# One encoder layer with 16 experts: the third expert list ahead moved behind the row transposes, and a head transpose moved behind the second pool product

## The chip, the cores and the metric

The kernel runs on one core of a Trainium2 chip. A core has a matrix engine (TensorE, called PE in the profile, with its weight loads as PEld), a vector engine (VectorE, DVE), a scalar engine (ScalarE, ACT), a general engine (GpSimd, POOL) and a queue engine (SyncE, SP). Each works through its own list of instructions in order. They meet only through semaphores. Transfers between the main memory and the on-chip buffers run on 16 DMA engines. SP and POOL issue them.

The metric is the device time of one execution in microseconds (us), and less is better. All times "from the start" are counted from the start of the profiled span.

## The reference

One layer for 576 tokens: 512 prompt rows and 64 rows of a running stream. The two groups are computed apart in the reference and together in the kernel.

```python
h = rmsnorm(x, g_mix); proj = h @ w_in                 # u, q, k, v
pool_out = multiscale_pool(u, ...)                     # 4 groups, each with its own 128x128 map
o = differential attention(q, k, v), 4 heads
x = x + concat([pool_out, attn_out]) @ w_out           # the out projection
h2 = rmsnorm(x, g_ffn)
expert_id, top_w = two of 16 experts for each token    # group of 4, then 2 in the group
for e in range(16):
    he = silu(h2 @ w_gate[e]) * (h2 @ w_up[e])         # 1024 -> 256
    moe = moe + combine[..., e:e+1] * (he @ w_down[e]) # 256 -> 1024
y = rmsnorm(x + moe, g_final)
```

## The kernel before

Each engine has a program written out by hand in one long function. The order of the instructions on an engine is the order of that code. A `wait_ge(semaphore, count)` holds the engine, with all that stands behind it, until another engine has counted that far.

**The out projection.** Tokens are worked in five tiles t = 0..4 of 128 (the last has 64). `project_out(t, half, features)` on PE multiplies one tile by one half (512 columns) of `w_out`. For each 128 features it makes three matmuls (lines 822, 823, 824), since both operands are split in a high and a low part. Features 0 to 3 are the pool outputs (`pools`), 4 to 7 the attention heads (`heads`). Four pool products stand among these calls. `pool_product(g)` (line 1014, two matmuls) writes banks 4 and 5 of PSUM. Before g > 0 it waits for `pool_evac`, which says that the banks have been read: first ACT writes the high part (line 1517) and then DVE the low part (`pool_lo`, line 1882). `transpose_o(3)` (line 986, four transposes) waits for `o_ready`, which DVE gives when it has scaled the attention rows of token tile 3 (`o_norm`, line 1813) with a factor that POOL makes in a chain of small steps (lines 645 to 655). ACT and DVE then write the transposed rows as high part (`oT_hi`, line 1491) and low part (`oT_lo`, line 1822).

**The expert loop.** 16 steps i = 0..15, unrolled for 0 to 3 and 12 to 15, a hardware loop between. An expert works on up to 128 token rows. Its tokens are named by a list that the kernel makes on the way:

- DVE makes a 0/1 table with the slots of the tokens (`expert_onehot`, line 2018).
- PE multiplies it with a table of token numbers and weights (`slot_lists` called by `lists_of`, line 1175, five small matmuls).
- DVE turns the product into the list (`lists_out`, lines 2122 and 2123), which counts `idx_ready`.
- POOL then issues an indirect DMA that fetches the rows (`gather_h2`, line 699, `region_x<-h_rows,lists`).

PE in step i: `gate_up` of expert i (line 1188, 64 matmuls), `transpose_rows` of the rows of expert i+1 (line 1181, eight transposes, waiting for the gather), `down_split` of expert i-1 (lines 1205, 1206, 1210) and `lists_of(3)`, the list of expert i+3. Step 1 makes two lists more, behind its `gate_up`. In step 1 `lists_of(3)` may not start before DVE has read the list of expert 2, since both use one PSUM bank.

DVE in step i: `he_out(i)` (lines 2129 to 2131, the product of gate and up), the one-hot table of expert i+3, from step 6 on `finish_row(i-2)` (lines 2152 to 2162, the final norm), `add_rows(i-1)` (line 2146: adds the weighted rows of expert i-1 to the sums gathered for them, so it waits for `down_split` and for a gather), `lists_out(i+3)`, `wd_los(i+1)` (line 2136). Step 0 ends with `count_overflow` (lines 2086 to 2112, 24 small instructions, once). Step 1 makes the lists of experts 2 and 3 besides.

POOL in step i, in this order: `gather_h2(i+3)`, from step 6 on two stores of finished rows (line 742, 743), `store_acc(i-1)` (waits for `add_rows`), `gather_acc(i+1)` (the sums that `add_rows(i+1)` needs). SP loads the weights of the experts up to four ahead: gate and up when the buffer is free behind `gate_up`, down behind `down_split`.

Of the kernel before, what the change touches and what calls it, by code (L numbers as in the profile page):

```python
# [54 lines left out]
E = G * EPG  # L55
# [10 lines left out]
EARLY = 3  # L66
# [21 lines left out]
def build(nc, x_prompt, x_sample, cache_k, cache_v, state_pool, g_mix, w_in, w_pool, pool_scale,  # L88
# [4 lines left out]
    with ctx:  # L93
# [712 lines left out]
        def _(pe):  # L806
# [277 lines left out]
            pool_product(0)  # L1084
            project_out(1, 0, heads[0:2])
            transpose_o(PT - 1)
            pool_product(1)
            project_out(1, 0, heads[2:4])
            project_out(1, 1, heads[0:1])
# [147 lines left out]
            def expert(it, u, left):  # L1237
# [21 lines left out]
                if first:  # L1259
                    pe.wait_ge(tab_ready, 1)  # L1260
                    for n in range(2):
                        lists_of(n)
                if not first and left != 0:
                    pe.wait_ge(he_ready, i)
                    if not (isinstance(it, int) and i == 1):
                        pe.wait_ge(added, i - 1)
                    pe.wait_ge(wd_lo_ready, i)
                    down_split((u - 1) % RING, i - 1, 4)
                if not first and (left is None or left >= EARLY):
                    lists_of(EARLY)  # L1270
                if left == 1:
# [45 lines left out]
        def _(act):  # L1317
# [197 lines left out]
            for g in range(H):  # L1515
                act.wait_ge(pool_full, g + 1)
                act.activation(two_halves(mix_hi[:, g, :]), ps[:, 4:6, 0:HALF], ACT.Copy,
                               scale=pscale[:, g:g + 1]).then_inc(pool_hi_ready, 1)
                if g == 0:
                    oT_hi(NT - 2)  # L1520
# [124 lines left out]
        def _(dve):  # L1645
# [239 lines left out]
            w_out_los(H)  # L1885
            w_out_los(H + 1)
            o_norm(NT - 2)
            pool_lo(0)
            w_out_los(H + 2)
# [281 lines left out]

            for i in range(E - 1):
                he_out(i)
                if i == 0:
# [3 lines left out]
                    lists_out(1)  # L2178
                if i == 1:
                    lists_out(2)  # L2180
                    lists_out(3)
                if i >= 1 and i + EARLY < E:
                    expert_onehot(i + EARLY)
                if i > RING + 1:
                    finish_row(i - 2)
                if i >= 1:
                    add_rows(i - 1)
                    if i + EARLY < E:
                        lists_out(i + EARLY)
                if i < E - 2:  # L2190
# [125 lines left out]
```

## Time and profile before

| | |
|---|---|
| device time, median of 3 runs | 452.24 us (451.46 to 453.07) |
| the profiled execution, its own time | 450.83 us |
| its span (first to last instruction in the trace) | 449.0 us |
| mean granted TensorE clock | 0.975 |
| PE busy | 421.5 us (94%) |
| DVE / ACT / POOL busy | 273.3 / 197.7 / 125.9 us |
| DMA moved | 91.36 MB, of it 18.93 MB by POOL's software queue |

PE is busy 94% of the span, so what matters is where PE waits, and where it runs at the lower of its clocks. In the trace's rows a bracket behind an instruction gives the idle time of its engine before it, and what ended it: `[1.50 <-DVE region_t L1813]` says that the engine was idle for 1.50 us until line 1813 of DVE had written region_t. Names like region_t stand for stretches of the on-chip memory that several tiles share. In the rows of this kernel region_x<-h_rows is the gather of token rows, ps is PSUM.

### The profile page before, as it was taken

What the parts mean: (1) busy time and instruction counts of PE and PEld (TensorE: products, weight loads), DVE (VectorE), ACT (ScalarE), POOL (GpSimd) and SP (SyncE); (2) the same over time, 40 slices, a digit from 0 to 9 for tenths busy, and PEclk for the clock granted to TensorE, in tenths of its full rate; (3) what the DMA queues carried; (4) which work ended last, traced back from release to release, by engine and by line L of the source; (5) the groups of instructions that cost most, each with busy time, mean ns of one, the idle gap of its engine ahead of it and who ended that gap; (6) DMA issues with size and microseconds to landing.
All of it is one profiled execution on the core that took longest, in us unless ns stands there. A gap on an engine that the chain in (4) does not pass through costs nothing.

```text
span 449.0 us, 7775 instructions
## 1 busy us (share of the span) xinstructions
PE 421.5 (94%) x2927; PEld 366.0 (82%) x2927; DVE 273.3 (61%) x655; ACT 197.7 (44%) x485; POOL 125.9 (28%) x207
## 2 busy tenths in 40 slices
PE   7899999999999998999998999999999998999970
PEld 3786999997876866888895988999999997899950
DVE  3855232616778987364258796555577775497770
ACT  6475222505576664232124433344455554366340
POOL 2010000200242415251001304333335543466431
PEclk9999999999999999999998999999999999899995
DMA  7841605306000089613226599998899999963120
GB/s 268 302 160 47 223 1 182 111 1 195 1 1 2 1 334 364 261 52 149 89 93 244 178 403 392 379 361 352 354 360 355 344 369 352 349 231 120 55 81 21
DMA packets 32073, 91.36 MB, mean 203 GB/s; under 512 B 11200, under 2 KB 11712, under 8 KB 27942
## 3 DMA queue, kind: packets, MB, share of 16 engines
q1 hardware_dynamic: 20790, 71.97, 43.4%
q0 software_dynamic: 11248, 18.93, 12.0%
q8 instruction: 21, 0.34, 0.3%
q14 instruction: 14, 0.11, 0.1%
HBM read 86.38 MB, written 26.01 MB: 250 GB/s over the span
## 4 chain that ended last, share of the span: by engine, by line
PE 61%; issue 12%; DVE 7%; POOL 7%; DMA 6%; ACT 5%; POOLq 0%; SPq 0%; DVEq 0%; ACTq 0%
PE ps L1188 13%; PE ps L822 9%; PE ps L824 9%; PE ps L823 9%; DMA region_x<-h_rows,lists 5%; PE ps L1125 2%; PE ps L1181 2%; PE ps L1205 2%; PE ps L1206 2%; PE ps L1210 2%; PE ps L943 2%; PE ps L978 2%; POOL region_x L699 2%; DMA region_x<-in_x_prompt 1%; POOL mix L699 1%
## 5 line engine op out<-in xcount | busy, mean ns | idle before, releaser
L1188 PE MATMUL ps<-region_p,region_a 128*128 128x128 f32 x512 | 59.1, 276 | 0.6 <-DVE region_p L2025 0.6
L1188 PEld LDWEIGHTS ps<-region_p,region_a 128*128 128x128 f32 x512 | 57.9, 192 | 1.2 <-DVE region_p L2025 1.1
L824 PE MATMUL ps<-region_a_r,region_w_r 128*128 128x288 f32 x192 | 56.5, 294 | 0.0
L699 POOL DMA_INDIRECT region_x<-h_rows,lists x13 | 22.1, 1700 | 77.6 <-DVE slot_w L2123 77.6
L822 PE MATMUL ps<-region_a_r,ring_r 128*128 128x288 f32 x128 | 40.5, 317 | 0.0
L823 PE MATMUL ps<-region_a_r,ring_r 128*128 128x288 f32 x128 | 37.7, 295 | 0.0
L1575 ACT ACTIVATE region_p<-ps,gffn_sb 128x128 f32<-128x128 f32 x116 | 31.5, 382 | 10.9 <-PE ps L1181 10.9
L824 PEld LDWEIGHTS ps<-region_a_r,region_w_r 128*128 128x128 f32 x192 | 36.1, 188 | 0.0
L1596 ACT ACTIVATE region_t<-ps 128x256 f32<-128x256 f32 x16 | 6.1, 382 | 56.1 <-PE ps L1188 56.1
L1188 PE MATMUL ps<-region_p,ring 128*128 128x128 f32 x256 | 29.6, 277 | 0.6 <-DVE region_p L2047 0.4
L822 PEld LDWEIGHTS ps<-region_a_r,ring_r 128*128 128x128 f32 x128 | 24.0, 188 | 6.9 <-issue 3.3
L1188 PEld LDWEIGHTS ps<-region_p,ring 128*128 128x128 f32 x256 | 28.9, 192 | 0.7 <-DVE region_p L2047 0.5
L1188 PE MATMUL ps<-region_p,region_w 128*128 128x128 f32 x256 | 29.5, 276 | 0.0
L2146 DVE SCALAR_TENSOR_TENSOR mix<-ps,slot_w,mix 128x1024 f32<-128x1024 f32 x15 | 19.2, 1282 | 16.4 <-DMA mix<-summed_rows,lists 10.8
L1188 PEld LDWEIGHTS ps<-region_p,region_w 128*128 128x128 f32 x256 | 29.0, 192 | 0.1
L1762 DVE TENSOR_SCALAR region_q<-ps 128x288 f32<-128x288 f32 x8 | 3.7, 458 | 39.8 <-PE ps L824 39.8
L2129 DVE TENSOR_TENSOR region_t_r<-region_t,ps 128x256 fp32r<-128x256 f32 x16 | 6.7, 421 | 32.7 <-ACT region_t L1596 32.7
L823 PE MATMUL ps<-region_w_r,mix_r 128*128 128x512 f32 x64 | 25.6, 399 | 0.0
L1205 PE MATMUL ps<-region_q_r,region_t_r 128*128 128x512 f32 x60 | 25.3, 421 | 0.0
L823 PEld LDWEIGHTS ps<-region_a_r,ring_r 128*128 128x128 f32 x128 | 24.1, 188 | 0.0
L1438 ACT ACTIVATE region_p<-ps,negm 128x128 f32<-128x128 f32 (+4 forms) x40 | 20.7, 527 | 5.8 <-DVE negm L1794 5.8
L1602 ACT ACTIVATE region_q<-mix 128x1024 f32<-128x1024 f32 x11 | 11.6, 1057 | 21.4 <-DVE mix L2146 21.4
(358 smaller groups left out, 1025.8 us busy)
## 6 DMA issues: line engine op xcount, KB each, us to landing
region_a<-in_w_gate SPq DMA_DIRECT2D x8, 1024.0 KB, 8.3
region_a<-in_w_up SPq DMA_DIRECT2D x8, 1024.0 KB, 13.2
region_a<-in_w_down SPq DMA_DIRECT2D x8, 1024.0 KB, 14.7
region_w<-in_w_in SPq DMA_DIRECT2D x2, 2048.0 KB, 10.2
region_w<-in_w_out SPq DMA_DIRECT2D x2, 2048.0 KB, 8.0
ring<-in_w_gate SPq DMA_DIRECT2D x4, 1024.0 KB, 9.2
ring<-in_w_up SPq DMA_DIRECT2D x4, 1024.0 KB, 13.9
ring<-in_w_down SPq DMA_DIRECT2D x4, 1024.0 KB, 13.1
```

The lines of the kernel that those rows point to most:

```text
L699: pool.indirect_dma_start(out=dst, out_offset=None, in_=src, in_offset=bass.IndirectOffsetOnAxis(ap=at, axis=0), bounds_check=bound[n], oo ...
L822: pe.matmul(out, lhs_hi, rhs_hi, start=first, stop=False)
L823: pe.matmul(out, lhs_hi, rhs_lo, start=False, stop=False)
L824: return pe.matmul(out, lhs_lo, rhs_hi, start=False, stop=last)
L943: ins = pe.matmul(ps[:, b + c, 0:(t + 1) * P], q, kT[r, h, 0:(t + 1) * P], start=True, stop=True)
L978: ins = pe.matmul(ps[0:m, O_BANK[t], h * VD:(h + 1) * VD], aT[0:keys, n % 2, k * P:k * P + m], v, start=(k == 0), stop=(k == len(tiles) - 1))
L1188: ins = pe.matmul(ps[:, 2 + b, (first + c) * P:(first + c + 1) * P], w[:, k, c * P:(c + 1) * P], xT[:, b, k, :], start=(k == 0), stop=(k = ...
L1205: pe.matmul(ps[:, bank + half, :], he_hi[:, b, c, :], w_hi[:, c, n], start=(c == 0), stop=False)
L1438: ins = act.activation(prob[0:m, n % 2, c, 0:w], ps[0:m, 2 * (n % 2) + c, 0:w], ACT.Exp, bias=negm[0:m, n % 2, c:c + 1], scale=-1.0, accum ...
L1575: return act.activation(xT[:, b, k, :], ps[:, k // 4, (k % 4) * P:(k % 4 + 1) * P], ACT.Copy, scale=gffn_sb[:, k:k + 1])
L1602: act.activation(squares, xacc[:, i % RING, :], ACT.Square, accum_out=ssq[:, i % 2:i % 2 + 1]).then_inc(squared, 1)
L2146: dve.scalar_tensor_tensor(acc, ps[:, bank:bank + 2, :], slot_w[:, w:w + 1], acc, ALU.mult, ALU.add).then_inc(added, 1)
```

## The change

Two parts. In the out projection the second half of `project_out(1, 0, heads)` moves ahead of pool product 1, and `transpose_o(3)` moves behind it. ACT and DVE follow in their order: `oT_hi(3)` behind the second pool product's high part, `pool_lo(0)` ahead of `o_norm(3)`.

In the expert loop PE makes `lists_of(3)` right behind `transpose_rows`, ahead of `down_split`. DVE makes the list right behind `he_out`, ahead of the one-hot table, `finish_row` and `add_rows`. The one-hot tables are made one step earlier, which puts that of expert 4 into step 0, and the lists of experts 2 and 3 stand ahead of `he_out(1)`.

```diff
             project_out(0, 1, heads[2:4])
             pool_product(0)
-            project_out(1, 0, heads[0:2])
+            project_out(1, 0, heads)
+            pool_product(1)
             transpose_o(PT - 1)
-            pool_product(1)
-            project_out(1, 0, heads[2:4])
             project_out(1, 1, heads[0:1])
             pool_product(2)
...
+                if not first and (left is None or left >= EARLY):
+                    lists_of(EARLY)
                 if not first and left != 0:
                     pe.wait_ge(he_ready, i)
...
                     down_split((u - 1) % RING, i - 1, 4)
-                if not first and (left is None or left >= EARLY):
-                    lists_of(EARLY)
...
-                if g == 0:
+                if g == 1:
                     oT_hi(NT - 2)
...
             w_out_los(H + 1)
+            pool_lo(0)
             o_norm(NT - 2)
-            pool_lo(0)
             w_out_los(H + 2)
...
             for i in range(E - 1):
+                if i == 1:
+                    lists_out(2)
+                    lists_out(3)
                 he_out(i)
                 if i == 0:
...
-                if i == 1:
-                    lists_out(2)
-                    lists_out(3)
-                if i >= 1 and i + EARLY < E:
-                    expert_onehot(i + EARLY)
+                elif i + EARLY < E:
+                    lists_out(i + EARLY)
+                if i + EARLY + 1 < E:
+                    expert_onehot(i + EARLY + 1)
                 if i > RING + 1:
                     finish_row(i - 2)
                 if i >= 1:
                     add_rows(i - 1)
-                    if i + EARLY < E:
-                        lists_out(i + EARLY)
```

PE in the out projection, from behind the first part of `project_out(1, 0, heads)` to pool product 2. L986 is `transpose_o(3)`, L1014 a pool product, L822 to L824 the projection. Before:

```order
L986 MATMUL ps<-ident,region_t 128x128 x4
L1014 MATMUL ps<-mix,region_x 128x288 x2
L822 MATMUL ps<-region_x_r,mix_r 128x512
L823 MATMUL ps<-region_w_r,mix_r 128x512
L824 MATMUL ps<-region_x_r,region_a_r 128x512
L822 MATMUL ps<-w_hi_extra,mix_r 128x512
L823 MATMUL ps<-region_w_r,mix_r 128x512
L824 MATMUL ps<-w_hi_extra,region_a_r 128x512
L822 MATMUL ps<-ring_r,mix_r 128x512
L823 MATMUL ps<-region_w_r,mix_r 128x512
L824 MATMUL ps<-ring_r,region_a_r 128x512
L1014 MATMUL ps<-mix,region_x 128x288 x2
```

After, the same stretch:

```order
L822 MATMUL ps<-region_x_r,mix_r 128x512
L823 MATMUL ps<-region_w_r,mix_r 128x512
L824 MATMUL ps<-region_x_r,region_a_r 128x512
L822 MATMUL ps<-w_hi_extra,mix_r 128x512
L823 MATMUL ps<-region_w_r,mix_r 128x512
L824 MATMUL ps<-w_hi_extra,region_a_r 128x512
L1014 MATMUL ps<-mix,region_x 128x288 x2
L986 MATMUL ps<-ident,region_t 128x128 x4
L822 MATMUL ps<-ring_r,mix_r 128x512
L823 MATMUL ps<-region_w_r,mix_r 128x512
L824 MATMUL ps<-ring_r,region_a_r 128x512
L1014 MATMUL ps<-mix,region_x 128x288 x2
```

Six projection matmuls stand ahead of pool product 1 now, the transposes stand behind it, and only three matmuls and the transposes stand between pool products 1 and 2.

PE in step 1 of the expert loop, from its `gate_up`. L1188 (L1187 after) is `gate_up`, L1175 (L1174) a list product, L1181 (L1180) `transpose_rows`, L1205 and L1206 (L1204 and L1205) the start of `down_split(0)`. Before:

```order
L1188 MATMUL ps<-region_p,region_a 128x128 x32
L1175 MATMUL ps<-region_q,region_v 128x8 x10
L1181 MATMUL ps<-ident,region_x 128x128 x8
L1205 MATMUL ps<-region_q_r,region_t_r 128x512
L1206 MATMUL ps<-ring_r,region_t_r 128x512
```

After:

```order
L1187 MATMUL ps<-region_p,region_a 128x128 x32
L1174 MATMUL ps<-region_q,region_v 128x8 x10
L1180 MATMUL ps<-ident,region_x 128x128 x8
L1174 MATMUL ps<-region_q,region_v 128x8 x5
L1204 MATMUL ps<-region_q_r,region_t_r 128x512
L1205 MATMUL ps<-ring_r,region_t_r 128x512
```

The list product x5 stood behind the whole of `down_split(0)` and stands ahead of it now.

DVE from the end of `count_overflow` (step 0) through step 1. L2129 to L2131 is `he_out(1)`, L2122 and L2123 are a list, L2018 is a one-hot table, L2146 `add_rows(0)`. Before:

```order
L2112 CAST ctl<-region_k 1x1
L2129 TENSOR_TENSOR region_t_r<-region_t,ps 128x256
L2130 TENSOR_TENSOR region_t<-region_t,ps 128x256
L2131 TENSOR_TENSOR region_t_r<-region_t,region_t_r 128x256
L2122 TENSOR_SCALAR lists<-ps 128x4
L2123 TENSOR_REDUCE slot_w<-ps 128x1
L2122 TENSOR_SCALAR lists<-ps 128x4
L2123 TENSOR_REDUCE slot_w<-ps 128x1
L2018 TENSOR_TENSOR region_v<-iota_one,rm 128x640
L2146 SCALAR_TENSOR_TENSOR mix<-ps,slot_w,mix 128x1024
L2122 TENSOR_SCALAR lists<-ps 128x4
L2123 TENSOR_REDUCE slot_w<-ps 128x1
```

After (each of these lines has a number lower by one):

```order
L2111 CAST ctl<-region_k 1x1
L2121 TENSOR_SCALAR lists<-ps 128x4
L2122 TENSOR_REDUCE slot_w<-ps 128x1
L2121 TENSOR_SCALAR lists<-ps 128x4
L2122 TENSOR_REDUCE slot_w<-ps 128x1
L2128 TENSOR_TENSOR region_t_r<-region_t,ps 128x256
L2129 TENSOR_TENSOR region_t<-region_t,ps 128x256
L2130 TENSOR_TENSOR region_t_r<-region_t,region_t_r 128x256
L2121 TENSOR_SCALAR lists<-ps 128x4
L2122 TENSOR_REDUCE slot_w<-ps 128x1
L2017 TENSOR_TENSOR region_v<-iota_one,rm 128x640
L2145 SCALAR_TENSOR_TENSOR mix<-ps,slot_w,mix 128x1024
```

The two lists stand ahead of `he_out(1)`, but still behind `count_overflow`; the list of expert 4 stands ahead of the one-hot table and `add_rows`. Ahead of `count_overflow` the one-hot table of expert 4 has come in, between the lists of step 0 and `wd_los(1)`:

```order
L2121 TENSOR_SCALAR lists<-ps 128x4
L2122 TENSOR_REDUCE slot_w<-ps 128x1
L2017 TENSOR_TENSOR region_v<-iota_one,rm 128x640
L2135 TENSOR_TENSOR region_a_r<-region_a,region_q_r 128x1024 x2
L2085 TENSOR_SCALAR region_k<-region_k 128x16
```

Before, no L2018 stood there.

## Rows read from the trace of the kernel before

**Rows 1.** The page: costliest groups (busy, mean ns | idle before) and DMA issues (us to landing).

```profile
L699 POOL DMA_INDIRECT region_x<-h_rows,lists x13 | 22.1, 1700 | 77.6 <-DVE slot_w L2123 77.6
...
region_a<-in_w_down SPq DMA_DIRECT2D x8, 1024.0 KB, 14.7
```

**Rows 2.** Timeline of PE in the out projection: start us, us, engine line op [idle before].

```profile
172.62 0.61 PE L822 MATMUL ps<-ring_r,mix_r 128*128 128x512 f32 x1
...
175.88 0.66 PE L986 MATMUL ps<-ident,region_t 128*128 128x128 f32 x4 [1.50 <-DVE region_t L1813]
176.70 1.35 PE L1014 MATMUL ps<-mix,region_x 128*128 128x288 f32 x4 [0.16 <-DVE region_a_r L1882]
...
181.40 1.13 PE L1014 MATMUL ps<-mix,region_x 128*128 128x288 f32 x4
182.16 0.61 PE L822 MATMUL ps<-ring_r,mix_r 128*128 128x512 f32 x1
...
184.46 1.13 PE L1014 MATMUL ps<-mix,region_x 128*128 128x288 f32 x4
185.21 0.61 PE L822 MATMUL ps<-region_p_r,mix_r 128*128 128x512 f32 x1
```

**Rows 3.** Timelines of DVE, then of ACT, in the same stretch.

```profile
175.14 0.69 DVE L1813 TENSOR_TENSOR region_t<-ps,osc 128x512 f32<-128x512 f32 x1 [1.49 <-POOL osc L655]
...
178.87 0.82 DVE L1882 SCALAR_TENSOR_TENSOR region_a_r<-ps,pscale,mix_r 128x576 fp32r<-128x576 f32 x1 [1.19 <-ACT mix_r L1517]
...
173.30 0.73 ACT L1517 ACTIVATE mix_r<-ps,pscale 128x576 fp32r<-128x576 f32 x1
...
178.09 0.74 ACT L1517 ACTIVATE mix_r<-ps,pscale 128x576 fp32r<-128x576 f32 x1 [0.83 <-PE ps L1014]
```

**Rows 4.** Windows: stretch, us, busy by engine, then PEclk, DMA share, GB/s.

```profile
176.50:181.50 5.00, 4.84 (x15) 3.80 (x15) 2.66 (x4) 1.43 (x2) 0.00 (x0) 0.66 0.97 378
```

**Rows 5.** Windows of four steps of the expert loop, from one gate_up to the next.

```profile
272.95:284.45 11.50, 11.23 (x94) 10.34 (x92) 5.59 (x9) 4.53 (x11) 4.44 (x4) 1.00 1.01 380
...
306.41:317.39 10.98, 10.98 (x95) 10.32 (x92) 5.67 (x9) 4.55 (x11) 3.77 (x3) 1.00 0.98 396
...
372.68:387.92 15.24, 12.81 (x95) 11.75 (x92) 9.94 (x23) 5.58 (x13) 7.07 (x6) 0.89 0.97 379
387.92:399.25 11.33, 11.23 (x95) 10.36 (x93) 6.27 (x15) 5.70 (x13) 4.50 (x4) 1.00 0.71 245
```

**Rows 6.** Timeline of PE in the expert loop: first rows behind its waits.

```profile
261.50 4.73 PE L1188 MATMUL ps<-region_p,region_a 128*128 128x128 f32 x40 [0.65 <-DVE region_p L2025]
...
280.62 1.09 PE L1181 MATMUL ps<-ident,region_x 128*128 128x128 f32 x8 [0.27 <-DMA region_x<-h_rows,lists]
...
382.50 1.97 PE L1181 MATMUL ps<-ident,region_x 128*128 128x128 f32 x8 [2.43 <-DMA region_x<-h_rows,lists]
```

**Rows 7.** Tile h_rows on POOL, 331 to 367: the four gathers for steps 8 to 11.

```profile
L699 POOL DMA_INDIRECT region_x<-h_rows,lists x4: 1727/1736/1738, 331.8 to 366.2; - x4
...
DMA to landing us min/median/max: 9.1/12.6/16.2
```

**Rows 8.** Timeline of DVE in the expert loop, steps 6 and 10.

```profile
326.03 0.42 DVE L2131 TENSOR_TENSOR region_t_r<-region_t,region_t_r 128x256 fp32r<-128x256 f32 x1
...
331.41 0.15 DVE L2123 TENSOR_REDUCE slot_w<-ps 128x1 f32<-128x3 f32 x1
...
378.85 1.28 DVE L2146 SCALAR_TENSOR_TENSOR mix<-ps,slot_w,mix 128x1024 f32<-128x1024 f32 x1 [4.39 <-DMA mix<-summed_rows,lists]
```

**Rows 9.** Timeline of DVE from the end of count_overflow, then of PE, step 1.

```profile
270.33 0.14 DVE L2112 CAST ctl<-region_k 1x1 int32<-1x1 f32 x1
...
271.67 0.15 DVE L2123 TENSOR_REDUCE slot_w<-ps 128x1 f32<-128x3 f32 x1
...
271.94 0.82 DVE L2018 TENSOR_TENSOR region_v<-iota_one,rm 128x640 bf16<-128x640 f32 x1
...
269.83 0.47 PE L1205 MATMUL ps<-region_q_r,region_t_r 128*128 128x512 f32 x1
```

## The prediction

> **What bounds the kernel now.** I read the busy times first: PE works 94% of the span, so the time is PE's work, plus its waits, plus what it loses at the lower clock. Then the page's groups, for who waits on whom: the gathers of token rows cost POOL little, but POOL idles 77.6 us in front of them, all of it for DVE's lists [rows 1]. The DMA issues give the landing of a weight load, 14.7 us for the down weights [rows 1]. Then PE's timeline at the two places that the change touches.
>
> In the out projection PE idles 1.50 us for the scaled head rows of tile 3 (line 1813) and 0.16 us for pool product 0's banks [rows 2]. DVE was not late by its own work there: it idled 1.49 us for POOL's factor [rows 3]. From 176.5 to 181.5 the granted clock is 0.66 of full [rows 4], which is a stretch at 1.2 GHz within one at 2.4 GHz. It follows that idle.
>
> In the expert loop an undisturbed step takes 10.98 us. Three steps take longer: step 2 11.50, step 11 15.24, step 12 11.33, that is 0.52 + 4.26 + 0.35 = 5.13 us too much [rows 5]. The rows behind the waits name the cause: the transposes of step 2 waited 0.27 us for their gather, those of step 11 2.43 us [rows 6]. Behind the second wait the clock fell too (0.89 in that step's window [rows 5], and the eight transposes took 1.97 us where they took 1.09 in step 2 [rows 6]). So of step 11's 4.26 us some 2.4 are waiting, and the other 1.8 (mainly the clock) come behind it. I take 1.6 us as what one fall of the clock costs PE in this loop.
>
> The gathers get later from step to step: from issue to landing 9.1 us for the first of the four behind 331, 16.2 us for the last, issued at 366.2 [rows 7]. That is (16.2 - 9.1) / 3 = 2.4 us a step, with the DMA engines at a share of 0.97 to 1.0 [rows 5]. The last lands at 366.2 + 16.2 = 382.4. PE was ready for it at 382.50 - 2.43 = 380.07 [rows 6].
>
> **Part 1, the out projection.** Before, the stretch from the projection at 172.62 to the projection with the pool features at 185.21 takes 12.59 us [rows 2]. What it takes now:
>
> - Nine projection matmuls take 184.46 - 182.16 = 2.30 us [rows 2]; twelve take 3.0. So pool product 1 can start at 172.62 + 3.0 = 175.6. Its banks are free by then: ACT has written the high part by 173.30 + 0.73 = 174.0, and DVE, idle until 175.14, can write the low part (0.82) by 174.9 [rows 3]. The wait of 0.16 goes.
> - A pool product takes 182.16 - 181.40 = 0.76 us until the next matmul starts [rows 2]. The transposes come at 176.4. Their rows are there at 175.88 [rows 2], because POOL's factor is as early as before. The wait of 1.50 goes: six matmuls and a pool product cover it.
> - The transposes and three matmuls end at about 177.7. Pool product 2 needs the banks of product 1. Product 1 takes 1.13 [rows 2] and is done at 176.7; then ACT's 0.74 and DVE's 0.82 in a row [rows 3] make 178.4 to 178.5. **A new wait of 0.8 us** stands there, where nine matmuls at the lower clock hid it before.
> - From pool product 2 to product 3 it is 184.46 - 181.40 = 3.06, and 0.75 more to the pool features [rows 2]: 178.5 + 3.06 + 0.75 = 182.3.
>
> Gain: 185.21 - 182.33 = **2.88 us**. It assumes that the wait of 0.8 does not bring the lower clock. If it does, the three matmuls behind it run as they do in the stretch of 0.66 [rows 4], and 1.6 us come back. Everything behind stands on PE, so the 2.88 shift the rest as a whole.
>
> **Part 2, the lists.** In step 6 `he_out` ends at 326.45 and the list at 331.56 [rows 8]. Between them stood the one-hot table, the final norm and `add_rows`. The list now comes right behind `he_out`: about 4.9 us earlier, and so does the gather that waits for it. In step 10 `add_rows` waited 4.39 us for a gather of its own [rows 8], which held the list of step 12's rows too; this hold goes as well. POOL's stores stand behind the gather and follow by some 3 us, as the final norm ends at nearly its old time.
>
> What the earlier issue is worth depends on the queue. If the transfer takes as long as before, step 11's rows land at 382.4 - 4.9 = 377.5, 2.6 us ahead of the need. It takes only 2.4 of the 4.9 to end that wait. Step 12 is the tighter one: its gather ended just as PE came for it, at a time when PE was 5 us late; to be in time without that delay, it must land about 4.3 us earlier than before. Bounds for what is left there: 0 and 2 us; I take 0.6, nearer to the low end, since its issue comes earlier by more than 4.9. So of the 5.13 us the change takes **4.5**. Step 2's part goes because PE comes there later now (next paragraph).
>
> **Part 2, the new wait in step 1.** This is the cost. `lists_of(3)` of step 1 needs the bank that DVE frees with the list of expert 2. This list stands behind `count_overflow`, which ends at 270.33 + 0.14 = 270.47 [rows 9]. The one-hot table of expert 4 now stands in front of all that, and DVE has no idle there: 0.8 us [rows 9] make it 271.25, and the two small instructions of a list 271.5. PE reaches the place where `down_split` started, 269.83 [rows 9], and stands until about 271.5 with the whole of `down_split(0)` and `gate_up(2)` queued behind. Cost: **1.65 us**. Before, the list product came 3 us later and waited for nothing.
>
> **The clock behind it.** The row of before is nearest in the two cases: an idle of 1.50 + 0.16 us [rows 2] was followed by the lower clock [rows 4], one of 2.43 us too; one of 0.65 us was not [rows 6]. A wait of 1.65 is nearer to the first. I take **1.6 us** for it; the other end is 0.
>
> Other edits: `lists_of(3)` and the one-hot tables only change places in the other steps. The list product needs a bank that was read a step ago and a table that was made a step ago, so PE waits for neither. The two lists ahead of `he_out(1)` delay `down_split(1)` by nothing, as that comes a step later. Bounds for the list product's place: 0.1 us a step either way over ten steps; I take 0.
>
> **Sum**, in the profiled execution: -2.88 - 4.53 + 1.65 + 1.6 = -4.16, so 450.83 - 4.16 = 446.7. That execution lies 1.41 us below the median of the three runs; against the median it is 452.24 - 4.16 = **448.1**.
>
> **The rivals.**
>
> - *The clock does not fall in step 1* (B): 448.1 - 1.6 = 446.5. For it: the wait stands at the edge of what the rows show.
> - *The clock falls at the new wait of 0.8* (E): 448.1 + 1.6 = 449.7. Against it: 0.65 us of idle brought nothing [rows 6].
> - *The queue and not the list sets when rows land* (C). For it: the gathers' time to land grows by 2.4 us a step, while PE and the lists keep their pace [rows 7], and the DMA engines are full [rows 5]. A gather issued earlier then only lies longer in the queue. I work it out with half the shift lost: step 11 keeps about 1.2 of its 2.43 us, step 12 up to 1, and one more fall of the clock comes in half the cases: 0.6 becomes 3.5, and the time 448.1 + 2.9 = 451.0. Against it: until 366 the gathers were issued only after the list, with POOL idle in front of them [rows 1], so the queue had time in which it was fed late.
> - *The gathers go ahead of the weights, and PE waits for weights* (D), which ends slower. Weights of down are asked for at the end of a step and needed two steps on, 22.0 us, and take 14.7 [rows 1]: 7.3 us of cover. If the 2.4 us a step that the gathers lost until now [rows 7] fall on the weights, three of the six steps from 6 on use up the cover, and the other three cost 2.4 us each, 7.1 in all, with one fall of the clock: -2.88 - 5.13 + 1.65 + 1.6 + 7.1 + 1.6 = +3.9, so 456.2. It decides from the point at which a weight load takes over 22 us. Against it: the cover is used up only if all of that growth changes sides.
>
> The Trainium skill, "DMA: Bandwidth & Descriptors", section "Queues, rings and completion order", says that each DMA engine goes in turns, packet by packet, through the queues for which it has work. By that rule POOL's queue keeps its share beside SP's weights however early it is filled, which is rival C, 451.0; this trace agrees in so far as the gathers slow down beside full engines, and does not show which queue gives way.
>
> **How the numbers follow.** A measurement of this kernel can tell about 0.3% from no change, 1.36 us. Chances: the forecast 448.1: 0.42; B 446.5: 0.24; E 449.7: 0.09; C 451.0: 0.18; D 456.2: 0.07. The range goes from B without the 0.6 and with 0.4 of the list product's bound, 445.5, to C with 0.4 of it, 451.4. D and the ends beyond are left out. Faster by over 0.3% (under 450.9): the forecast, B, E and about a third of C, 0.80. Within: the rest of C, 0.13. Slower: D, 0.07.
>
> **What would show it.** Right: no wait at line 986's transposes, a wait of about 0.8 us at pool product 2 for `pool_lo(1)`; in step 1 a wait of 1.4 to 1.7 us at the list product (L1174) for DVE's list, and the clock low behind it; no wait over 0.5 us at the transposes of steps 2 and 11; lists about 5 us earlier against `gate_up`. Wrong: the transposes of step 11 still wait over 1 us (C), `gate_up` waits for weights (D), the first part gains under 2 us because the clock falls there (E), or the stretch at the lower clock comes at another place of the loop that none of these rows shows.

## The result: 446.1 us, and the profile after

The changed kernel takes 446.14 us (median of 4 runs, 444.89 to 447.15) where the kernel before takes 452.65 us beside it: a ratio of 0.9848, 95% interval 0.9814 to 0.9883. A second set of runs, on another occasion (e5 below), gives 446.6 against 451.22 us, a ratio of 0.9884, interval 0.985 to 0.9918. So the change saves some 4.6 to 6.5 us by the medians. 448.1 us had been forecast, 2 us too much; the rival without a lower clock in step 1, 446.5 us, lies nearest. The times alone do not decide between the two, since they stand for gains of 4.2 and 5.8 us; the traces do.

The page of the changed kernel, its span and the group of the gathers:

```profile
span 443.2 us, 7774 instructions
...
L699 POOL DMA_INDIRECT region_x<-h_rows,lists x13 | 16.6, 1280 | 48.6 <-DVE slot_w L2122 48.2
```

The profiled execution is 5.8 us shorter in its span. POOL idles 48.6 us ahead of the gathers where it idled 77.6 [rows 1]: the lists do come earlier.

PE's timeline in the out projection, the rows that answer to [rows 2]:

```profile
172.33 0.61 PE L822 MATMUL ps<-ring_r,mix_r 128*128 128x512 f32 x1
...
175.31 1.13 PE L1014 MATMUL ps<-mix,region_x 128*128 128x288 f32 x4
176.28 0.60 PE L986 MATMUL ps<-ident,region_t 128*128 128x128 f32 x4
...
178.23 1.21 PE L1014 MATMUL ps<-mix,region_x 128*128 128x288 f32 x4 [0.65 <-DVE region_a_r L1881]
...
181.32 1.13 PE L1014 MATMUL ps<-mix,region_x 128*128 128x288 f32 x4
182.08 0.61 PE L822 MATMUL ps<-region_p_r,mix_r 128*128 128x512 f32 x1
```

The transposes (L986) have no idle in front of them. The wait has moved to pool product 2 and is 0.65 us long. The stretch takes 182.08 - 172.33 = 9.75 us; it took 12.59.

Windows of that stretch and of steps 1, 2, 11 and 12 of the expert loop (stretch, us, busy by engine, PEclk, DMA share, GB/s), the answer to [rows 5]:

```profile
172.33:182.08 9.75, 9.10 (x43) 7.05 (x41) 6.99 (x8) 3.47 (x5) 3.28 (x8) 1.00 1.02 374
258.36:271.40 13.04, 11.56 (x100) 10.83 (x101) 11.20 (x45) 3.63 (x11) 2.31 (x2) 1.00 0.99 399
271.40:282.37 10.97, 10.97 (x90) 10.47 (x89) 5.67 (x9) 4.55 (x11) 3.57 (x3) 1.00 0.95 366
370.24:381.22 10.98, 10.98 (x91) 10.47 (x90) 7.76 (x16) 5.59 (x13) 4.80 (x5) 1.00 0.93 348
381.22:393.44 12.22, 11.18 (x90) 10.50 (x89) 8.69 (x24) 5.58 (x13) 6.30 (x6) 1.00 0.86 335
```

Steps 2 and 11 are down to an undisturbed step, from 11.50 and 15.24. Step 12 has got longer, from 11.33 to 12.22. Step 1 takes 13.04; before, from 261.50 to 272.95, it took 11.45 [rows 6, 5]. The granted clock is 1.00 in all five: no stretch at 1.2 GHz among them.

The waits in steps 1 and 12 in PE's timeline, the gather that step 12 waits for in POOL's, and the end of `count_overflow` with the list behind it in DVE's:

```profile
268.41 0.27 PE L1174 MATMUL ps<-region_q,region_v 128*128 128x8 bf16 x5 [1.48 <-DVE slot_w L2122]
...
389.56 1.09 PE L1180 MATMUL ps<-ident,region_x 128*128 128x128 f32 x8 [1.04 <-DMA region_x<-h_rows,lists]
...
368.70 1.34 POOL L699 DMA_INDIRECT region_x<-h_rows,lists  x1 [1.74 <-DVE slot_w L2122]
...
267.93 0.14 DVE L2111 CAST ctl<-region_k 1x1 int32<-1x1 f32 x1
...
268.13 0.14 DVE L2122 TENSOR_REDUCE slot_w<-ps 128x1 f32<-128x3 f32 x1
```

The list product of step 1 waits 1.48 us for the list of expert 2, which DVE finishes at 268.27, right behind `count_overflow`. The gather for step 12 is issued at 368.70. By the end of PE's wait for it, it lands some 20.8 us later. The same gather in POOL's timeline before, and its time to landing there:

```profile
380.60 1.74 POOL L699 DMA_INDIRECT region_x<-h_rows,lists  x1 [6.95 <-DVE slot_w L2123]
...
DMA to landing us min/median/max: 14.8/14.8/14.8
```

The balance of the spans (449.0 to 443.2, -5.8): out projection -2.84; step 1 +1.59; step 2 -0.53; steps 3 to 10 together -0.36; step 11 -4.26; step 12 +0.89; another -0.28 lies ahead of all that, at the start. Some 3.4 us of the -5.8 are the two stretches at 1.2 GHz (at 177 and 382 us) that the trace before has and this one does not.

### The profile page after: what moved, and what is told of

Same layout as the page of the kernel before. It is cut to its first block, busy times and chain, and to the rows that moved or that the text cites. A ratio compares the mean times of both kernels' runs of the same rounds, so it can differ in the third digit from the quotient of the medians.

```text
span 443.2 us, 7774 instructions
## 1 busy us (share of the span) xinstructions
PE 417.2 (94%) x2926; PEld 365.2 (82%) x2927; DVE 273.6 (62%) x655; ACT 197.6 (45%) x485; POOL 125.0 (28%) x207
## 4 chain that ended last, share of the span: by engine, by line
PE 64%; DVE 16%; DMA 7%; issue 6%; ACT 4%; POOL 0%; POOLq 0%; SPq 0%; DVEq 0%; ACTq 0%
PE ps L1187 13%; PE ps L822 10%; PE ps L824 9%; PE ps L823 9%; DMA region_x<-h_rows,lists 5%; PE ps L978 2%; PE ps L1204 2%; PE ps L1205 2%; PE ps L1209 2%; PE ps L1124 2%; PE ps L943 2%; PE ps L1180 1%; DMA region_w<-in_w_in 1%; DMA out_y_sample<-region_x,lists 1%; PE ps L961 1%
## 5 line engine op out<-in xcount | busy, mean ns | idle before, releaser
L1187 PEld LDWEIGHTS ps<-region_p,region_a 128*128 128x128 f32 x512 | 58.3, 192 | 1.7 <-DVE region_p L2024 1.1
L1187 PE MATMUL ps<-region_p,region_a 128*128 128x128 f32 x512 | 58.5, 275 | 0.7 <-DVE region_p L2024 0.7
L824 PE MATMUL ps<-region_a_r,region_w_r 128*128 128x288 f32 x192 | 56.5, 294 | 0.0
L822 PE MATMUL ps<-region_a_r,ring_r 128*128 128x288 f32 x128 | 40.5, 317 | 0.0
L824 PEld LDWEIGHTS ps<-region_a_r,region_w_r 128*128 128x128 f32 x192 | 36.0, 188 | 0.0
L699 POOL DMA_INDIRECT region_x<-h_rows,lists x13 | 16.6, 1280 | 48.6 <-DVE slot_w L2122 48.2
L1187 PEld LDWEIGHTS ps<-region_p,ring 128*128 128x128 f32 x256 | 29.1, 192 | 0.8 <-DVE region_p L2046 0.5
L1187 PE MATMUL ps<-region_p,ring 128*128 128x128 f32 x256 | 29.3, 275 | 0.4 <-DVE region_p L2046 0.4
L822 PEld LDWEIGHTS ps<-region_a_r,ring_r 128*128 128x128 f32 x128 | 24.0, 188 | 6.9 <-issue 3.3
L1187 PEld LDWEIGHTS ps<-region_p,region_w 128*128 128x128 f32 x256 | 29.2, 192 | 0.3
L1187 PE MATMUL ps<-region_p,region_w 128*128 128x128 f32 x256 | 29.2, 275 | 0.0
L2145 DVE SCALAR_TENSOR_TENSOR mix<-ps,slot_w,mix 128x1024 f32<-128x1024 f32 x15 | 19.2, 1282 | 11.1 <-PE ps L1209 6.2
L1204 PE MATMUL ps<-region_q_r,region_t_r 128*128 128x512 f32 x60 | 24.7, 411 | 0.0
L704 POOL DMA_INDIRECT out_y_prompt<-region_x,lists x12 | 12.0, 1002 | 35.8 <-DVE region_x L2161 32.7
```

Source lines behind the costliest of these rows:

```text
L699: pool.indirect_dma_start(out=dst, out_offset=None, in_=src, in_offset=bass.IndirectOffsetOnAxis(ap=at, axis=0), bounds_check=bound[n], oo ...
L704: pool.indirect_dma_start(out=dst, out_offset=bass.IndirectOffsetOnAxis(ap=at, axis=0), in_=src, in_offset=None, bounds_check=bound[n], oo ...
L822: pe.matmul(out, lhs_hi, rhs_hi, start=first, stop=False)
L824: return pe.matmul(out, lhs_lo, rhs_hi, start=False, stop=last)
L1187: ins = pe.matmul(ps[:, 2 + b, (first + c) * P:(first + c + 1) * P], w[:, k, c * P:(c + 1) * P], xT[:, b, k, :], start=(k == 0), stop=(k = ...
L1204: pe.matmul(ps[:, bank + half, :], he_hi[:, b, c, :], w_hi[:, c, n], start=(c == 0), stop=False)
```

## The experiments

Each comparison is with the kernel before, run beside it. There are three sets: e1 to e4 (before 451.82 us), e5 to e8 (451.22 us), e9 to e11 (451.49 us). Executions of one kernel differ by 3 to 7 us. Part of that goes with the clock: over the 57 executions of the kernel before, span and mean granted clock have a correlation of -0.54. The mean clock over a kernel's executions is therefore given too. For the kernel before it is 0.9788, 0.9792 and 0.9798 in the three sets.

| | what it is | median us | ratio (95%) | mean clock |
|---|---|---|---|---|
| e1 | out projection alone | 450.72 | 0.9988 (0.9957 to 1.0018) | 0.981 |
| e2 | lists alone | 449.0 | 0.9942 (0.9915 to 0.997) | 0.982 |
| e5 | whole change again | 446.6 | 0.9884 (0.985 to 0.9918) | 0.985 |
| e9 | whole, longer wait in step 1 | 450.44 | 0.9959 (0.9936 to 0.9982) | 0.978 |
| e10 | whole, step 1 undone | 445.25 | 0.9845 (0.982 to 0.987) | 0.985 |
| e3 | whole, count_overflow later | 444.9 | 0.9863 (0.9831 to 0.9896) | 0.985 |
| e8 | whole, last weights later | 445.22 | 0.9862 (0.9825 to 0.9899) | 0.985 |
| e4 | both of these | 443.18 | 0.9841 (0.9809 to 0.9874) | 0.986 |
| e11 | e4 again | 443.12 | 0.9814 (0.9783 to 0.9845) | 0.983 |
| e6 | before, PE busy in its wait | 451.05 | 1.0 (0.9967 to 1.0032) | 0.981 |
| e7 | before, most of y not stored | 446.13 | 0.9893 (0.985 to 0.9937) | 0.983 |

### The two parts apart (e1, e2)

e1 takes the first part alone, e2 the second; their diffs are the halves of the change's.

> Only the first part of the change: the order of project_out, pool product 1 and transpose_o(3), with ACT and DVE following. The lists stay as before. Theory: the stretch from the projection behind pool product 0 to the first projection with the pool features falls from 12.59 us to 9.75 us, everything behind moves as a whole, and the waits of steps 2, 11 and 12 of the expert loop stay (5.1 us too much). Span 449.0 - 2.8 = 446.2, time 2.8 us under the kernel before. Rival: the expert loop's transfers do not move with PE, so that part of the 2.8 us comes back as longer waits there: under 2 us gained.

Windows of e1 (the stretch of the out projection, steps 11 and 12), then the window of e2's out projection in the old order, then the wait there in e2's PE timeline:

```profile
172.94:182.69 9.75, 9.10 (x42) 7.05 (x41) 6.98 (x8) 3.49 (x5) 3.29 (x8) 1.00 1.02 366
...
369.45:382.81 13.36, 11.24 (x96) 10.35 (x92) 8.87 (x22) 5.60 (x13) 5.84 (x5) 1.00 0.96 377
382.81:395.90 13.09, 11.23 (x95) 10.34 (x92) 7.29 (x15) 5.60 (x13) 5.68 (x5) 1.00 0.72 261
```

```profile
174.32:185.33 11.01, 9.35 (x42) 7.09 (x41) 6.91 (x8) 3.59 (x5) 2.44 (x8) 1.00 1.02 365
```

```profile
177.58 0.66 PE L986 MATMUL ps<-ident,region_t 128*128 128x128 f32 x4 [1.50 <-DVE region_t L1813]
```

> Only the second part: the lists on PE and DVE. The out projection as before. Theory: 1.5 us of new wait in step 1, no wait at the transposes of steps 2 and 11, about 1 us at those of step 12; the clock stays high in step 1. Span 449.0 - 3.0 = 446.0. Rival: the new wait in step 1 is followed by the lower clock once PE's activity in front of it is that of the kernel before, then 1.6 us less is gained: 447.6.

In e1 the stretch is 9.75 us, as expected, but the gain in time is 1.1 us by the medians and not told from none by the interval. e2's trace says why the gain can be that small: there the old order, with the same 1.50 us of wait, takes 11.01 us and not 12.59, for the clock stays at 2.4 GHz behind it. **So the first part saves 11.01 - 9.75 = 1.26 us where the clock stays up, and 1.6 more only where it would have fallen**, which it did in one of the three traces with this wait (before, e2, e7). Steps 11 and 12 of e1 show the same for the loop: in the order before, without a fall of the clock, the two steps are 2.4 and 2.1 us too long (two waits for gathers), where [rows 5] showed 4.3 and 0.35. The rival of this run, that PE comes too early for its gathers because of the first part, does not explain them: e6 (below) has the out projection in the old order, and its steps 11 and 12 are 1.9 and 2.2 us too long:

```profile
371.10:384.01 12.91, 11.23 (x96) 10.35 (x92) 8.64 (x21) 5.59 (x13) 5.55 (x5) 1.00 0.95 377
384.01:397.19 13.18, 11.22 (x96) 10.35 (x92) 7.57 (x17) 5.58 (x13) 6.02 (x5) 1.00 0.71 271
```

e2 gains 2.8 us, near to the 3.0 expected, with the wait of 1.5 us in step 1 and no lower clock behind it in its trace. Its steps 12 and 13 wait 1.09 and 1.61 us for gathers; only the first had been expected. The parts add up to 3.9 us by the medians, the whole to 4.6 (e5); the intervals are too wide to make anything of the difference.

### The whole change again (e5)

> The whole change once more, on the chip and beside the runs of the kernel before that e6 to e8 have, for its share of executions with stretches at the lower clock. Theory (waits and clock): the waits gained are 1.27 us in the out projection and some 2 to 3 us in the expert loop, the same in every execution; the rest of the gain is clock, which falls at 176 us and at the wait of step 11 only in some executions of the kernel before and has no such wait to fall at here. Then its mean clock is 0.004 to 0.006 above that of the kernel before and its median 5 to 6.5 us under it. Rival (waits alone): mean clock equal, 4 us under it.

Gain 4.6 us by the medians, mean clock 0.0053 over that of the kernel before in its set, so the rival with equal clocks is out. One stretch at the lower clock, 3.4 us long in the records, lowers a run's mean clock by 0.0038 and costs 1.6 us (12.59 - 11.01). By that, some 2.2 us of the 4.6 are clock, an estimate, and the rest waits. The traces give a similar sum for the waits, 2.8 us: 1.26 in the out projection, and in the loop e1 has 5.5 us of excess in steps 2, 7, 11 and 12, e5 1.5 in step 1 and 2.4 in steps 12 and 13.

That the 2.2 us come from the two waits that the change removes is not shown. A mean clock counts every stretch of an execution, and only the profiled executions tell where they lie. Ten of the thirteen traces have one between 238 and 246 us, ahead of the expert loop, and four (e2, e3, e5, e10) have one between 12 and 18 us; the change moves nothing at either place. The changed kernel's window, with the granted clock at 0.66:

```profile
238.00:243.00 5.00, 4.71 (x31) 2.66 (x32) 3.79 (x25) 3.97 (x6) 1.73 (x2) 0.66 0.96 383
```

### The wait in step 1 and the clock behind it (e9, e10, e3)

e9 makes the wait longer, with two one-hot tables more (`False`: they do not count the semaphore that PE waits for):

```diff
+                if i == 0:
+                    for _ in range(2):
+                        expert_onehot(i + EARLY + 1, False)
                 if i + EARLY + 1 < E:
                     expert_onehot(i + EARLY + 1)
```

> The whole change with two more one-hot tables written ahead of the one of expert 4 in step 0 (the same table over again, 0.8 us each, one behind the other), so that count_overflow and the list of expert 2 come 1.6 to 1.8 us later and PE's wait in step 1 is 3.1 to 3.3 us in place of 1.48. It asks whether the size of the wait decides on the clock there, as the prediction had it. If it does, the clock falls behind this wait in every execution: 1.7 + 1.6 = 3.3 us over e5_whole_again, mean clock 0.004 lower. If not, 1.7 us over it and the mean clock as there, 0.984; part of the 1.7 may be given back at the transposes of steps 12 and 13.

e9's PE timeline at the wait, and behind it the window from its end to `gate_up(2)`:

```profile
272.29 0.27 PE L1174 MATMUL ps<-region_q,region_v 128*128 128x8 bf16 x5 [3.18 <-DVE slot_w L2126]
...
272.73 0.39 PE L1205 MATMUL ps<-ring_r,region_t_r 128*128 128x512 f32 x1
...
274.98 0.63 PE L1205 MATMUL ps<-ring_r,region_t_r 128*128 128x512 f32 x1
```

```profile
272.29:276.83 4.54, 4.54 (x18) 3.64 (x19) 2.08 (x7) 0.00 (x0) 2.31 (x2) 0.62 0.95 393
```

In this trace the clock falls right behind the wait: matmuls of one shape take 0.39 and then 0.63 us, and the granted clock of the window is 0.62. The stretch from the list product to `gate_up(2)` takes 4.54 us where it takes 271.40 - 268.41 = 2.99 in the changed kernel: 1.55 us, as the prediction had priced a fall. The median is 3.8 us over e5, which is of another set, and the mean clock 0.007 lower. Not all of that is the fall in step 1: the same trace has a stretch at 1.2 GHz of 6.8 us from 239 us on, where the changed kernel has one of 3.4. And the fall need not come in every execution: the fastest of the twelve takes 446.28 us at a mean clock of 0.986.

Behind 1.46 to 1.48 us, in the four traces that have this wait (after, e2, e5, e8), the clock does not fall. So the price was right, for a fall that did not come. What decides between the cases is not shown.

e10 puts the list product of step 1 back, and e3 moves what is in its way:

```diff
-                if not first and (left is None or left >= EARLY):
+                late = isinstance(it, int) and i == 1
+                if not first and not late and (left is None or left >= EARLY):
                     lists_of(EARLY)
...
                     down_split((u - 1) % RING, i - 1, 4)
+                if late:
+                    lists_of(EARLY)
```

```diff
                     expert_onehot(i + EARLY + 1)
+                if i == 1:
+                    count_overflow()
...
-                if i == 0:
-                    count_overflow()
```

> The whole change, but the list product of step 1 stands behind down_split(0) again, as in the kernel before; everything else as changed. It measures the new wait by itself. Theory: the wait of 1.48 us goes, step 1 takes 11.4 us in place of 13.0; part of it comes back in step 2, whose rows land at the same time and are now needed 1.6 us earlier: 0.5 to 0.9 us of wait at its transposes. Median 0.7 to 1.1 us under e5_whole_again. Rival: all of 1.6 us is gained.

> The whole change, with count_overflow (24 small DVE instructions) moved from the end of step 0 to step 1, behind the one-hot table of expert 5 and ahead of add_rows(0), where DVE waits for down_split(0) anyway. Theory: the list of expert 2 no longer stands behind it, PE's wait of 1.48 us at the list product of step 1 goes, and nothing takes its place: span 443.2 - 1.6 = 441.6. Rival: the DMA engines set when the rows of the late steps land, so what PE gains in step 1 comes back as a longer wait at the transposes of step 11 or 12 (1.04 us at step 12 becomes 2.6): span as with the whole change, 443.2.

Windows of steps 1 and 2 in e10, the transposes of step 2 in its PE timeline, and the two windows in e3:

```profile
260.60:271.91 11.31, 11.31 (x100) 10.62 (x100) 10.27 (x42) 3.65 (x11) 0.93 (x1) 1.00 1.01 411
271.91:283.73 11.82, 11.28 (x96) 10.59 (x93) 6.69 (x12) 4.55 (x11) 4.89 (x5) 1.00 1.00 386
```

```profile
279.84 1.09 PE L1180 MATMUL ps<-ident,region_x 128*128 128x128 f32 x8 [0.54 <-DMA region_x<-h_rows,lists]
```

```profile
261.15:272.55 11.40, 11.40 (x100) 10.86 (x101) 6.95 (x24) 3.62 (x11) 2.32 (x2) 1.00 1.00 399
272.55:284.48 11.93, 11.19 (x91) 10.50 (x89) 9.84 (x31) 4.55 (x11) 3.56 (x3) 1.00 1.00 383
```

In both the wait of step 1 is gone (the step is 1.6 to 1.7 us shorter), and about half of it is back in step 2 (0.84 and 0.95 us over 10.98). The rows of step 2 land no earlier: its transposes start, behind a wait for them, 19.2 us (e10) and 19.4 us (e3) after step 1 starts, and 19.1 us in the kernel before [rows 6]. The medians are 1.4 us (e10) and 1.7 us (e3) under e5, but of other sets and with intervals that overlap; it is the traces that show the exchange. The rival of e3, that all comes back later, is out: step 12 waits 1.19 us where it waited 1.04, and step 11 does not wait. The expected gain of 1.6 without anything in its place is not what the trace shows either.

### List or queue (e7, e8, e4, e11)

e7 is the kernel before, in which the stores of finished rows carry 2 rows in place of 128, so most of y isn't written:

```diff
-                rows_to(yp_rows, N_PROMPT, lists[:, i % LISTS, 2:3], yf[:, i % 2, :], stored)
-                rows_to(ys_v, N_SAMPLE, lists[:, i % LISTS, 3:4], yf[:, i % 2, :], stored)
+                rows_to(yp_rows, N_PROMPT, lists[0:2, i % LISTS, 2:3], yf[0:2, i % 2, :], stored)
+                rows_to(ys_v, N_SAMPLE, lists[0:2, i % LISTS, 3:4], yf[0:2, i % 2, :], stored)
```

> The kernel before, lists as they were, but the stores of finished rows in the expert loop move 2 rows in place of 128 (their issue and semaphores stay), so most of y is left out. It tells the list's part from the queue's. If the late rows of steps 11 and 12 come from POOL's queue, filled by those stores from step 6 on, the gathers land after 9 to 10 us in every step and the waits of steps 11 and 12 go: span 449.0 - 4.6 = 444.4. If they come from the late issue (the list) alone, the waits of some 2 us stay.

Windows of its steps 11 and 12:

```profile
371.56:382.56 11.00, 11.00 (x96) 10.32 (x92) 8.28 (x19) 5.70 (x13) 6.04 (x5) 1.00 0.96 378
382.56:393.56 11.00, 11.00 (x96) 10.31 (x92) 8.28 (x19) 5.70 (x13) 6.04 (x5) 1.00 0.80 314
```

Both steps are undisturbed, with the lists where they stood in DVE's order. The gather for step 12 in its POOL timeline:

```profile
374.99 1.74 POOL L699 DMA_INDIRECT region_x<-h_rows,lists  x1 [3.74 <-DVE slot_w L2123]
```

That is 14.4 us behind the start of step 10 (360.56). In the kernel before it is 18.9 us (380.60 - 361.68), in the changed one 9.4 us (368.70 - 359.26). So the old place of the list does not make the rows late by itself; the late rows of steps 11 and 12 need the load of the y stores. That load works in two ways, and e7 takes both away at once: the gather lies longer in the queue, and `add_rows` of step 10 waits 4.39 us for a gather of its own [rows 8], which held the next list behind it. In e7 `add_rows` waits for nothing there. How much either way costs is not told apart. The change moves the list out from behind `add_rows`, so the second way is closed, and the earlier issue meets the first.

e8 takes load from the queue's neighbour: SP asks for the last expert's gate and up weights one step later.

```diff
             for i in range(E - RING):
-                sp.wait_ge(up_full, i + 1)
-                load_gate_up(i % RING, expert_at(i + RING))
+                last = i == E - RING - 1
+                if not last:
+                    sp.wait_ge(up_full, i + 1)
+                    load_gate_up(i % RING, expert_at(i + RING))
                 if i >= 1:
                     sp.wait_ge(down_done, 2 * i)
                     load_down((i - 1) % RING, expert_at(i - 1 + RING))
+                if last:
+                    sp.wait_ge(up_full, i + 2)
+                    load_gate_up(i % RING, expert_at(i + RING))
```

> The whole change, and the gate and up weights of the last expert asked for 11 us later, behind gate_up(12); count_overflow stays in step 0. If weights and gathers share the DMA engines, the wait of 1.0 us at the transposes of step 12 goes to under 0.4, and the median is 0.7 to 1.2 us under e5_whole_again. If POOL's queue is bound by itself, the wait and the time stay.

`gate_up` of steps 12 and 13 in e8's PE timeline, then the transposes of the same steps in e5's:

```profile
382.18 7.30 PE L1192 MATMUL ps<-region_p,ring 128*128 128x128 f32 x64
393.16 7.30 PE L1192 MATMUL ps<-region_p,region_a 128*128 128x128 f32 x64
```

```profile
391.15 1.09 PE L1180 MATMUL ps<-ident,region_x 128*128 128x128 f32 x8 [0.37 <-DMA region_x<-h_rows,lists]
...
403.88 1.09 PE L1180 MATMUL ps<-ident,region_x 128*128 128x128 f32 x8 [1.55 <-DMA region_x<-h_rows,lists]
```

Step 12 takes 10.98 us: its wait is gone. In e5, beside it, steps 12 and 13 wait 0.37 and 1.55 us. The median is 1.4 us under e5; the intervals of the two overlap, so it is the trace that shows the wait's end. Together with e4 and e11 below it says that POOL's queue does gain when the weights are held back.

e4 and e11 are one kernel, e3 and e8 together:

> As e3_count_late, and the gate and up weights of the last expert are asked for behind gate_up(12) in place of gate_up(11), 11 us later; they are needed in step 15. Nothing is left out. It tells which of the two queues gives way. If POOL's queue gets the share of the DMA engines that the weights leave free, the gather for step 12 lands 1 us or more earlier and its wait of about 1.04 us goes: 1.2 us under e3_count_late, span 440.4. If POOL's queue is bound by itself (its own packets, whatever the weights do), the wait stays and the span is that of e3_count_late.

> The kernel of e4_hold_weights once more (whole change, count_overflow in step 1, the last expert's gate and up weights asked for 11 us later), on the chip and beside the runs of the kernel before that e9 and e10 have. Theory: 2 to 3 us under e5_whole_again, 1.6 to 1.9% under the kernel before. Rival: without the lower-clock stretches by chance, no better than e10.

e11's windows of steps 1 and 12:

```profile
259.35:270.71 11.36, 11.36 (x99) 10.85 (x100) 6.91 (x24) 3.62 (x11) 2.32 (x2) 1.00 0.98 398
380.53:391.62 11.09, 11.09 (x91) 10.50 (x89) 8.04 (x21) 5.71 (x13) 5.75 (x5) 1.00 0.79 297
```

Neither the wait of step 1 nor that of step 12 is left. In e4's trace a part of the second is:

```profile
385.89 1.09 PE L1185 MATMUL ps<-ident,region_x 128*128 128x128 f32 x8 [0.35 <-DMA region_x<-h_rows,lists]
```

This is the fastest version found: 443.1 us, 3.5 us under e5 by the medians of different sets, 1.6% (e4) and 1.9% (e11) under the kernel before. The rival of e11, fewer stretches at the lower clock by chance, does not explain it: e11 is 2.1 us under e10 of the same set at a lower mean clock (0.983 against 0.985).

### The wait of the out projection filled with work (e6)

```diff
             project_out(1, 0, heads[0:2])
+            keep_running(6, 3)
             transpose_o(PT - 1)
```

> The kernel before with six matmuls of constants (bank 3, whose sums are overwritten later) put ahead of transpose_o(3), so that PE works through most of its 1.5 us wait there; the order and the wait stay. Nothing of the result is changed. If the fall of the clock at 177 us comes from that wait, no execution has it any more: mean clock up by some 0.002 (one stretch of 3.4 us is 0.0038 of the span), median about 0.5 to 1 us lower. If the fall has another source, clock and time stay as before.

e6's PE timeline:

```profile
174.61 1.47 PE L880 MATMUL ps<-ones 128*128 128x512 bf16 x6
176.26 0.66 PE L986 MATMUL ps<-ident,region_t 128*128 128x128 f32 x4 [0.19 <-DVE region_t L1814]
```

PE is busy through the wait and the clock does not fall there in this trace, as it did not in e2 and e7 with the wait left idle. The median stays (451.05 against 451.22), and the mean clock is 0.0016 higher, which is within the scatter of the executions. This run is inconclusive: it says only that the fall at 177 us costs less than about 1.5 us on the average over executions, by the interval's lower end (0.0033 of 451).

## Why the prediction came out as it did

**The out projection, right as a sum of the profiled execution, wrong as a saving of every one.** -2.88 was forecast, -2.84 measured in the trace. The new wait was put at 0.8 us and is 0.65; in none of the nine traces that have it does the clock fall there, so rival E did not come. What failed is that the 12.59 us of [rows 2] were taken as the stretch's usual time. They hold 1.6 us of a fall of the clock that e2 and e7 don't have with the same wait. The lasting part is 1.26 us.

**The lists: direction right, the remainder too small.** Steps 2 and 11 lost their waits. The list was put 4.9 us earlier against its step; by the gathers it is 5.0 in step 6 and 9.5 in step 10. Step 12 was called the tighter one with a remainder of 0 to 2 us, taken as 0.6; in step 12 it is 1.24 over an undisturbed step. In other executions it falls on steps 12 and 13 and leaves the bounds: 2.4 us in e5, 3.1 in e2; there is none in e8. Here too 1.8 of the 4.26 us of step 11 were mainly clock: e1's steps 11 and 12 are 4.5 us too long together where [rows 5] had 4.6, so in the sum it made little difference.

**The new wait of step 1, right.** 1.65 forecast, 1.48 idle and 1.59 on the step measured; e10 shows that the list product's place makes it. As the prediction said, it hides the wait of step 2; without it about half of the 1.6 us comes back there (e10, e3).

**The clock behind it, wrong.** +1.6 was taken, on the ground that the wait is nearer to 1.50 + 0.16 than to 0.65 us. In four traces the clock does not fall behind 1.46 to 1.48 us; it does behind 3.18 in e9's, and then costs 1.55. The step that failed is the choice of the nearest row: the wait of 1.50 + 0.16 was itself a case that goes both ways, which one trace can't show. With this term at nothing the forecast would have been 446.5, against 446.14 and 446.6 measured. That it comes so near is in part luck: it counts the falls at 177 and 382 us, some 3.4 us, as saved in full, and the two measured gains are 1.9 us apart.

**The queue (rival C), half right as a mechanism.** The gather for step 12 was issued 11.9 us earlier (368.70 for 380.60), and landed only some 6 earlier (at about 389.5 for 395.4): it took 20.8 us for 14.8. Counted from the start of step 12 its rows came at 8.3 us, before at 7.5. So for this gather the queue did set the time, as C had it with half the shift lost. e7 shows that the y stores make the rows late. But the earlier issue was enough for step 11 with all of that load. Rival D, weights late, did not come: no trace has `gate_up` waiting for weights. The price of C was added up wrongly: its terms, 1.2 and 1 and half of 1.6, make 3.0 and not 3.5, so 450.5 and not 451.0.

The Trainium skill's rule that was cited ("DMA: Bandwidth & Descriptors", section "Queues, rings and completion order": each DMA engine serves its queues in turns) fits e8, where the wait for POOL's gather in step 12 is gone as soon as SP's weights are out of the way. The time that it was feared to bring (451.0) did not come: of the terms of that price only the remainder of step 12 is seen (in e5 and e2 partly in step 13), while step 11 waits no more and no further fall of the clock follows.

**The steps between.** Steps 3 to 10 became 0.36 us shorter, 0.29 of it step 7, which took 11.27 us from 328.39 on and takes 10.98 now. It is 11.23 to 11.27 in the four traces with the old lists and 10.98 in the nine with the new ones, so it belongs to the lists; why is not shown. It had been counted as staying.

## What to carry to other kernels

Where an instruction moves ahead in one engine's order, look up what frees the buffer that it writes, and what stands in front of that on the other engine: here a one-time block of 24 small instructions made a wait of 1.5 us, and moving that block into another idle took the wait away, of which about half came back in the next step. Take the time of a wait and the time of a lower clock behind it apart, and don't count the second as saved from one trace. Ask of an earlier issue how much earlier the data lands: here a gather issued 11.9 us earlier landed some 6 us earlier, and holding back a weight load that wasn't needed yet took the rest of the wait.

## What the runs showed that was not expected

- The same wait is followed by a lower clock in one execution and not in another: behind 1.50 us in the trace before, not in e2 and e7; behind 2.43 us in step 11 in the trace before, not behind 2.12 and 1.86 in steps 11 and 12 of e1, nor 1.68 and 1.96 in those of e6. Behind 1.46 to 1.48 us in step 1 it stayed at 2.4 GHz in all four traces, behind 3.18 us it fell to 1.2 GHz.
- The mean granted clock of single executions of the kernel before lies between 0.972 and 0.986. At 0.972 the spans are 451.4 to 451.5 us, at 0.986 447.8 to 448.5, but at 0.975 they go from 447.8 to 452.4: the clock is one part of the scatter, and the waits for gathers differ too. A change of 0.3% needs many executions here.
